# A two-layer block on one core: the recurrent stage fed with x as it stands, its products scaled afterwards

## The reference, cut to what matters

```python
def rg_lru(x, w_r, b_r, w_i, b_i, lam):
    r = sigmoid(block_diag_linear(x, w_r, b_r))
    i = sigmoid(block_diag_linear(x, w_i, b_i))
    log_a = -8.0 * r * softplus(-lam)
    a = exp(log_a)
    u = sqrt(-expm1(2.0 * log_a)) * (i * x)
    # h_t = a_t * h_(t-1) + u_t over the tokens
def hybrid_layer(x, ...):
    h = rmsnorm(x, g_mix)                  # x * rsqrt(mean(x*x) + eps) * g
    z = h @ w_in
    rnn_x, rnn_y, conv_b, conv_c, conv_x, gate_rnn, gate_conv = split(z)
    rnn_x = causal_depthwise_conv(rnn_x, conv4_w) + conv4_b
    y_rnn = gelu(rnn_y) * rg_lru(rnn_x, ...)
    y_conv = conv_b * causal_depthwise_conv(conv_c * conv_x, conv3_w)
    merged = sigmoid(gate_rnn) * y_rnn + sigmoid(gate_conv) * y_conv
    x = x + merged @ w_out
    ...                                    # a gated feed-forward, then an embedding gate
```

## Time and profile before

| what | value |
|---|---|
| median of 3 runs | 976.36 us (975.74 to 976.37) |
| the profiled execution's own time | 975.19 us |
| its span, first to last instruction | 973.4 us |
| PE busy in the span | 942.3 us |
| DVE busy | 741.0 us |
| ACT busy | 622.4 us |
| mean granted TensorE clock | 0.989 of full |
| bytes read from HBM | 213.03 MB |

### The profile page before, as it was taken

The page is one execution under the profiler, slowest core; times in us unless marked ns, Lnnn a source line. Parts: engine busy times, 40 slices in busy tenths (PEclk is TensorE's granted clock), DMA queues, the critical chain, the costliest instruction groups (busy, mean ns, idle before and its releaser), DMA issues.

```text
span 973.4 us, 13805 instructions
## 1 busy us (share of the span) xinstructions
PE 942.3 (97%) x5019; PEld 813.1 (84%) x5019; DVE 741.0 (76%) x1085; ACT 622.4 (64%) x949; POOL 20.5 (2%) x40
## 2 busy tenths in 40 slices
PE   7999999989899999999999799999999999999996
PEld 6888888878788888888888799999997888888875
DVE  5557686368799999999998778889797554555575
ACT  6685684566488877878777856756565643444455
POOL 2400000000000000000000000000000000000000
PEclk9999999999899999999999999999999999999999
DMA  9655325236199999999998264747466555555521
GB/s 339 200 187 199 130 92 212 87 99 223 70 360 368 359 369 370 350 365 371 335 371 305 82 206 148 228 128 237 151 215 203 200 180 183 187 190 174 202 99 43
DMA packets 102651, 214.64 MB, mean 221 GB/s; under 512 B 5629, under 2 KB 60177, under 8 KB 96977
## 3 DMA queue, kind: packets, MB, share of 16 engines
q1 hardware_dynamic: 101056, 211.83, 62.4%
q0 software_dynamic: 1392, 2.20, 0.8%
q10 hardware_dynamic: 160, 0.07, 0.0%
HBM read 213.03 MB, written 1.05 MB: 220 GB/s over the span
## 4 chain that ended last, share of the span: by engine, by line
PE 89%; DVE 5%; ACT 3%; issue 1%; DMA 1%; SPq 0%; DVEq 0%; ACTq 0%
PE bank L2113 21%; PE bank L2115 21%; PE bank L2114 21%; PE bank L2656 6%; PE bank L2657 6%; PE bank L2658 6%; PE bank L2118 4%; DVE w_lo L436 1%; DVE w_lo L438 1%; DMA xs<-in_mem_dram 1%; DVE xT_lo L1456 1%; PE bank L2443 1%; PE bank L2444 0%; ACT arena L924 0%; PE bank L2669 0%
## 5 line engine op out<-in xcount | busy, mean ns | idle before, releaser
L2113 PE MATMUL bank<-w_hi,xT_hi 128*128 128x512 f32 (+1 forms) x704 | 280.5, 398 | 1.6 <-DVE xT_lo L1456 1.0
L2115 PE MATMUL bank<-w_hi,xT_lo 128*128 128x512 f32 (+1 forms) x704 | 274.9, 390 | 0.0
L2114 PE MATMUL bank<-w_lo,xT_hi 128*128 128x512 f32 (+1 forms) x704 | 274.5, 390 | 0.0
L2113 PEld LDWEIGHTS bank<-w_hi,xT_hi 128*128 128x128 f32 x704 | 133.1, 189 | 29.0 <-issue 2.1
L2115 PEld LDWEIGHTS bank<-w_hi,xT_lo 128*128 128x128 f32 x704 | 132.4, 188 | 27.8
L2114 PEld LDWEIGHTS bank<-w_lo,xT_hi 128*128 128x128 f32 x704 | 132.8, 189 | 25.3
L436 DVE TENSOR_TENSOR w_lo<-stage,w_hi 128x1024 fp32r<-128x1024 f32 (+3 forms) x101 | 115.7, 1146 | 36.9 <-ACT w_hi L422 36.0
L2656 PE MATMUL bank<-xT_hi,w_hi 128*128 128x256 f32 x448 | 127.0, 284 | 0.0
L2657 PE MATMUL bank<-xT_lo,w_hi 128*128 128x256 f32 x448 | 126.8, 283 | 0.0
L2658 PE MATMUL bank<-xT_hi,w_lo 128*128 128x256 f32 x448 | 126.8, 283 | 0.0
L422 ACT ACTIVATE w_hi<-stage 128x1024 fp32r<-128x1024 f32 (+3 forms) x102 | 101.8, 998 | 37.3 <-PE bank L2658 18.8
(11 more groups left out here) (405 smaller groups left out, 1358.1 us busy)
## 6 DMA issues: line engine op xcount, KB each, us to landing
stage<-in_w_in_dram SPq DMA_DIRECT2D x36, 1024.0 KB, 5.1
stage<-in_w_gate_up_dram SPq DMA_DIRECT2D x44, 512.0 KB, 4.4
more<-in_expert_w_down_dram SPq DMA_DIRECT2D x17, 1024.0 KB, 6.6
stage<-in_expert_w_gate_dram SPq DMA_DIRECT2D x33, 512.0 KB, 5.1
stage<-in_expert_w_up_dram SPq DMA_DIRECT2D x33, 512.0 KB, 6.1
more<-in_expert_w_gate_dram SPq DMA_DIRECT2D x31, 512.0 KB, 5.0
more<-in_expert_w_up_dram SPq DMA_DIRECT2D x31, 512.0 KB, 5.9
stage<-in_expert_w_down_dram SPq DMA_DIRECT2D x15, 1024.0 KB, 6.7
```

Of the source, the lines that this page charges most:

```text
L2113: mm(o, k_hi, v_hi, start=start, stop=False)
L2114: mm(o, k_hi, v_lo, start=False, stop=False)
L2115: return mm(o, k_lo, v_hi, start=False, stop=stop)
```

## The change

- PE transposes `x` itself, two banks after two of the four additions and two after four. The squares, the mean and `rstd` are taken beside that and behind it. `rstd` is spread to a row of tokens (`row_wide`), transposed by PE inside the first GELU unit into a bank `scales`, and kept as `scale_row` (and its square `scale_row2`) in `xs`.
- In the heads, each product is multiplied by `scale_row` (a tensor_tensor over 512 columns whose second operand is read twice): RX into `xpad` by DVE in place of ACT's copy; GELU into `y_in` by DVE in place of ACT's copy; C times X in `cpad`, by the square, added; B's part in `conv3`, added; the gates G_R and G_C by DVE into `gr_tanh` and `gc_tanh`, which ACT then turns into tanh in place.
- The decay is ACT's Exp of `r_tanh` with scale and bias `decay_rate`, two instructions. On DVE the two reciprocals, the addition before them and the affine step behind them go, and one affine step (`q_inv`) comes. The polynomial of gelu has one tensor_scalar less. The split of G_C stands ahead of the decay's step.
- At the end of the experts, both chunks of the last down weights are split on ACT before the last tanh, and U_HEADS and U_HEADS + 1 (the first RX and GELU) before and behind `aT_hi`; DVE splits U_HEADS whole ahead of `sums`, and U_HEADS + 1 behind the `xT_lo` parts. In `down_by_chunks` and `bring_back` the matmuls that need only high parts come first.
- PE's first head is written out ahead of the loop, which then has three passes. POOL's load of `p_in` waits for the first `rx_hi`.

```diff
@@ ACT, end of the experts
+                if last_down_unit is not None:
+                    for c in range(2):
+                        chunk_hi(act, last_down_unit, c, st)
                 act.wait_ge(st.unit_done, g * PER_TURN + (up_unit(base, j) + 1))
...
-                if last_down_unit is not None:
-                    for c in range(2):
-                        chunk_hi(act, last_down_unit, c, st)
+                if last_down_unit is not None and splits[0]:
+                    splits[0]()
                 act.wait_ge(sem(name + "_turned"), eighths(g, j + 1))
                 nc.scalar.activation(flat3(aT_hi[:])[:, 0:FF], bank[7][:, 0:FF], ACT.Copy).then_inc(sem(name + "_aT_hi"), 1)
+                if last_down_unit is not None and splits[1]:
+                    splits[1]()
@@ ACT, the turn
         warm_up(ACT.Sqrt)
-        for c in range(2):
-            for t in range(T):
...
+        mix_squares(0, 0)
+        high_parts("mix", MIX_G)
+        mix_squares(0, 1)
+        mix_squares(1, 0)
+        mix_squares(1, 1).then_inc(sem("norm_sums"), 1)
         roots("mix")
-        for t in range(T):
-            nc.scalar.activation(xs[:, t, 512:1024], x[:, t, 512:1024], ACT.Copy, scale=rstd[:, t:t + 1]).then_inc(sem("mix_right"), 1)
-        high_parts("mix", MIX_G)
-        split_hi(act, SLOT, U_HEADS + 1)
@@ ACT, the heads
-            done(RX)
-            nc.scalar.activation(xpad[:, :, 3:259], blocks(bank[0]), ACT.Copy).then_inc(sem("rx_copied"), 1)
...
-            nc.scalar.activation(y_sq[:], bank[1][:, :], ACT.Square)
-            nc.scalar.activation(y_in[:], bank[1][:, :], ACT.Copy).then_inc(sem("y_copied"), 1)
+            act.wait_ge(sem("y_scaled"), h + 1)
+            nc.scalar.activation(y_sq[:], y_in[:], ACT.Square, scale=float(np.sqrt(0.044715))).then_inc(sem("y_squared"), 1)
...
+            for f in range(2):
+                rate = decay_rate[:, bass.ds(h * 2 + f, 1)]
+                nc.scalar.activation(decay_a[:, 256 * f:256 * f + 256], r_tanh[:, f], ACT.Exp, scale=rate, bias=rate)
...
-            done(G_R)
-            nc.scalar.activation(gr_tanh[:], bank[5][:, :], ACT.Tanh, scale=0.5).then_inc(sem("gr_tanh"), 1)
+            act.wait_ge(sem("gates_scaled"), h * 2 + 1)
+            nc.scalar.activation(gr_tanh[:], gr_tanh[:], ACT.Tanh, scale=0.5).then_inc(sem("gr_tanh"), 1)
             split_hi(act, SLOT, U_HEADS + 10, UNITS_HEAD, h)
-            done(G_C)
-            nc.scalar.activation(gc_tanh[:], bank[6][:, :], ACT.Tanh, scale=0.5).then_inc(sem("gc_tanh"), 1)
+            act.wait_ge(sem("gates_scaled"), h * 2 + 2)
+            nc.scalar.activation(gc_tanh[:], gc_tanh[:], ACT.Tanh, scale=0.5).then_inc(sem("gc_tanh"), 1)
@@ DVE, the heads
+            def scaled(dst, src, row):
+                return tt(by_feature(dst[:]), by_feature(src[:, :]), over_both(row), ALU.mult)
...
             unit(C_CONV)
+            done(RX)
+            tt(xpad[:, :, 3:259], by_feature(bank[0][:, :]), over_both(scale_row), ALU.mult).then_inc(sem("rx_copied"), 1)
...
-            link(ts(y_sq[:], y_sq[:], 0.044715, 1.0, ALU.mult, ALU.add))
-            tt(y_sq[:], y_sq[:], y_in[:], ALU.mult).then_inc(sem("gelu_inner"), 1)
+            done(GELU)
+            scaled(y_in, bank[1], scale_row).then_inc(sem("y_scaled"), 1)
             unit(RG_R)
+            dve.wait_ge(sem("y_squared"), h + 1)
+            stt(y_sq[:], y_sq[:], 1.0, y_in[:], ALU.add, ALU.mult).then_inc(sem("gelu_inner"), 1)
...
+            link(tt(cpad[:, :, 2:258], cpad[:, :, 2:258], over_both(scale_row2), ALU.mult))
...
+            unit(G_C)
             dve.wait_ge(sem("tau"), h * 2 + 2)
-            tf = tau[:].rearrange("p f t -> p (f t)")
-            link(ts(q_inv[:], tf, 1.0, None, ALU.add))
-            nc.vector.reciprocal(q_inv[:, 0:256], q_inv[:, 0:256])
-            unit(G_C)
-            link(nc.vector.reciprocal(q_inv[:, 256:512], q_inv[:, 256:512]))
-            ts(decay_a[:], q_inv[:], 2.0, -1.0, ALU.mult, ALU.add)
+            ts(q_inv[:], decay_a[:], 0.5, 0.5, ALU.mult, ALU.add)
             split_lo(dve, SLOT, U_HEADS + 9, UNITS_HEAD, h)
+            done(G_R)
+            scaled(gr_tanh, bank[5], scale_row).then_inc(sem("gates_scaled"), 1)
             done(B_CONV)
             y_conv = conv3[:].rearrange("p f t -> p (f t)")
-            tt(y_conv, bank[4][:, :], y_conv, ALU.mult)
+            link(tt(y_conv, bank[4][:, :], y_conv, ALU.mult))
+            tt(conv3[:], conv3[:], over_both(scale_row), ALU.mult)
...
+            done(G_C)
+            scaled(gc_tanh, bank[6], scale_row).then_inc(sem("gates_scaled"), 1)
             split_lo(dve, SLOT, U_HEADS + 10, UNITS_HEAD, h)
@@ PE
-        turn("mix", xs, [("mix_scaled", T)], (0, 1))
-        turn("mix", xs, [("mix_right", T)], (2, 3))
-        pe.wait_ge(sem("x_moe"), 4)
-        with pe.Fori(0, HEADS) as h:
+        turn("mix", x, [("x_moe", 2)], (0, 1))
+        turn("mix", x, [("x_moe", 4)], (2, 3))
...
+        head(0, first=True)
+        with pe.Fori(1, HEADS) as h:
+            head(h)
```

More of the change, by code:

```diff
@@ L1291, in read_flag, with early_head_split @@
             over_flag.append(overflow(act))
-        def early_head_split():
+        def early_head_split(u):
             with act.If(over_flag[0] < 1):
-                split_hi(act, SLOT, U_HEADS)
-        experts("moe", main, U_MOE, GROUPS, 1, read_flag, early_head_split)
+                split_hi(act, SLOT, u)
+        experts("moe", main, U_MOE, GROUPS, 1, read_flag, [lambda u=u: early_head_split(u) for u in (U_HEADS, U_HEADS + 1)])
         with act.If(over_flag[0] > 0):
@@ L1335, in _ @@
             nc.scalar.activation(rx_hi[:], rx[:].rearrange("p f t -> p (f t)"), ACT.Copy).then_inc(sem("rx_hi"), 1)
-            done(GELU)
-            nc.scalar.activation(y_sq[:], bank[1][:, :], ACT.Square)
-            nc.scalar.activation(y_in[:], bank[1][:, :], ACT.Copy).then_inc(sem("y_copied"), 1)
             unit(RG_R)
+            act.wait_ge(sem("y_scaled"), h + 1)
+            nc.scalar.activation(y_sq[:], y_in[:], ACT.Square, scale=float(np.sqrt(0.044715))).then_inc(sem("y_squared"), 1)
+            done(C_CONV)
+            nc.scalar.activation(c_in[:], bank[2][:, :], ACT.Copy).then_inc(sem("c_copied"), 1)
             act.wait_ge(sem("gelu_inner"), h + 1)
             nc.scalar.activation(y_tanh[:], y_sq[:], ACT.Tanh, scale=float(np.sqrt(2 / np.pi))).then_inc(sem("gelu_tanh"), 1)
-            done(C_CONV)
-            nc.scalar.activation(c_in[:], bank[2][:, :], ACT.Copy).then_inc(sem("c_copied"), 1)
             unit(B_CONV)
@@ L1864, in hidden_low @@
                    ALU.subtract).then_inc(sem(name + "_aT_lo"), 1)
-                if last_down_unit is not None:
-                    chunk_lo(dve, last_down_unit, 1, st).then_inc(st.lo_ready, 1)
             def sums(g):
@@ L1952, in _ @@
         dve.wait_ge(sem("padded"), 1)
+        b = product(dve, "scales")
+        then(nc.vector.tensor_copy(scale_row, b[:, 0:256]))
+        ins = tt(scale_row2, scale_row, scale_row, ALU.mult)
+        frees(ins, "scales")
+        been_read(dve, "scales")
         with dve.Fori(0, HEADS) as h:
@@ L2499, in down_by_chunks @@
                 s = u0 % RING
-                pe.wait_ge(sem(name + "_aT_lo"), eighths(g, LAST + 1))
+                hi, lo = (flat3(v[:]) for v in (aT_hi, aT_lo))
                 for c in range(2):
-                    if c:
-                        pe.wait_ge(st.lo_ready, u0 + 1)
+                    o, at = bank[4 + c][:, :], [D * k + 512 * c for k in range(2)]
+                    pe.wait_ge(sem(name + "_aT_hi"), eighths(g, LAST + 1))
                     for k in range(2):
-                        ins = down_block(LAST, s, k, c)
+                        mm(o, hi[:, P * k:P * k + P], w_hi[:, s, at[k]:at[k] + 512], start=False, stop=False)
+                    pe.wait_ge(sem(name + "_aT_lo"), eighths(g, LAST + 1))
+                    pe.wait_ge(st.lo_ready, u0 + 1)
+                    for k in range(2):
+                        mm(o, lo[:, P * k:P * k + P], w_hi[:, s, at[k]:at[k] + 512], start=False, stop=False)
+                        ins = mm(o, hi[:, P * k:P * k + P], w_lo[:, s, at[k]:at[k] + 512], start=False, stop=k == 1)
                     ins.then_inc(st.unit_done if c else sem("last_chunk"), 1)
@@ L2639, in swiglu, with turn_scales, head @@
             down(steps - 1, base + 3 * steps - 1, 0, 0, last_step=True)
-        turn("mix", xs, [("mix_scaled", T)], (0, 1))
-        turn("mix", xs, [("mix_right", T)], (2, 3))
-        pe.wait_ge(sem("x_moe"), 4)
-        with pe.Fori(0, HEADS) as h:
+        turn("mix", x, [("x_moe", 2)], (0, 1))
+        turn("mix", x, [("x_moe", 4)], (2, 3))
+        def turn_scales():
+            pe.wait_ge(sem("row_wide"), 1)
+            b = to_fill(pe, "scales")
+            for t in range(T):
+                ins = transpose(b[:, P * t:P * t + P], row_wide[:, t])
+            fills(ins, "scales")
+        def head(h, first=False):
```

(4 more changed lines are left out.)

78 lines of the change are left out of this document (38 added, 40 removed).

## The result

The changed kernel takes 981.51 us (median of 5 runs, 980.44 to 981.91) against 976.36 before (median of 5, 975.74 to 976.70): a ratio of 1.0052, 95% interval 1.0041 to 1.0064. It is 5.1 us slower, where 975.8 was forecast with a range up to 978.4. The profiled execution has 981.17 us of its own and a span of 979.4, 6.0 above that of before.

What follows compares the result with a forecast made beforehand. PE, busy 97% of the span, was taken to bound the kernel, gaining only where idle or low-clocked. Terms -4.8 + 4.3 = -0.5 against the profiled 975.19; with the median 1.2 above that, 975.8 us, range 971.6 to 978.4.

Steps and rivals of the forecast that it cites:

- Term 1: Turn from experts to heads: xT parts and PE's first unit start earlier; -4.8 us, bounds -4.0 to -5.3.
- step (2): Turn: PE transposes at 541.7 and from 542.95, so the xT_hi parts start at 542.45, 4.8 us earlier.
- Term 2: Heads: PE waits 1.25 us in each of heads 2 to 4, plus 0.3 and 0.24; +4.3 us.
- C: Turn: the norm's chain wasn't what held PE, term 1 given back at the weights' first split; about 980 us, chance 0.02.
- A: Heads: DVE doesn't bind and PE isn't held; 971.8 us, chance 0.19 with what lies between it and the main case.
- D: Heads: the loops bind harder, each missed 0.1 us costing 0.3; 0.8 per head gives 978.2 us, chance 0.10.
- B: Turn: clock falls as PE works in pieces with gaps, costing up to 3.0 us; 978.5 us, chance 0.07.

Runs made afterwards that it cites:

- e11: Kernel before the change with only the split of each next head's third weight unit (C_CONV) moved to the loop's end: 976.62 us.
- e2: Changed kernel with SP's load of the first head's X_CONV weight unit held back until the mixed x is split: 980.53 us.
- e1: Changed kernel with TensorE's branch over the overflow block taken out: 976.29 us.
- e3: Kernel before the change with TensorE's branch over the overflow block taken out: 976.02 us.
- e9: Kernel before the change with the decay part alone: decay by ScalarE's exponential, without the two reciprocals; turn and norm as they were: 975.27 us.
- e13: Changed kernel with the block behind TensorE's branch filled with 240 products in place of the overflow expert's: 981.94 us.
- e4: Changed kernel with TensorE's read of the overflow flag moved ahead of the last expert's steps, the jump left in place: 981.16 us.
- e7: Changed kernel, branch as it is, with the split of each next head's third weight unit (C_CONV) moved to the loop's end: 977.09 us.
- e10: Changed kernel with the two reciprocals put back for the exponential, the norm's factors still applied to the products: 984.84 us.
- e14: Changed kernel with the block behind TensorE's branch filled with 480 products in place of the overflow expert's: 981.83 us.
- e12: Changed kernel with the block behind TensorE's branch filled with 120 products in place of the overflow expert's: 976.92 us.
- e5: Changed kernel with TensorE's branch kept but the block it jumps over cut to its two waits: 976.51 us.
- e6: Changed kernel with TensorE's program behind the branch written twice, so that the no-overflow case falls through and all work is kept: 975.86 us.

## Why the prediction was wrong

**Term 1, the turn (-4.8): failed, at one step.** It was step (2), "PE transposes at 541.7". I took the profile's wait for `xs`, 3.9 us, as all that held PE, and listed what PE needs in data. The instruction ahead of the transposes is a jump over the overflow expert, and neither the chain nor the waits show it as long as a later wait covers it. Its end in the kernel before, about 545.5 by the packet, left 0.6 us to be gained (nothing in e11), and the weight load that the change lets through, worth 0.75 us in e2, takes that back. All else in the step was right: without the jump (e1 against e3) the transposes start 4.45 us earlier (forecast 4.4), the first product 5.00 (forecast 4.8), at a full clock. With the jump, the way from `aT_hi` to the first product is 13.59 us where it was 13.55.

**Term 2, the heads (+4.3): right in mechanism and place, undersized.** From the first product to ACT's first `xT_hi` behind the heads it takes 199.64 us in e1 (from 544.91) and 194.71 in e3 (from 549.91): +4.9.

```profile
744.55 0.85 ACT xT_hi L911 x2
744.62 0.85 ACT xT_hi L901 x2
```

Each loop cost 44.57 - 43.19 = 1.38 in place of 1.25, together 0.4 more. The other 0.2 lies in the first head and at the edges: there PE waits 0.5 us for DVE's splits, where I had 0.3 (and my own two times, 562.4 and 562.2, give only 0.2). The price of 0.12 for the link held: `conv`'s scaling starts 0.72 behind its linked predecessor (634.65, 635.37), where an unlinked one starts 0.60 behind.

**The sum.** -4.8 + 4.3 became 0.0 + 4.85 in the profiles (550.08 to 749.70 against 549.18 to 743.95 for the second). Of the span's 6.0, another 0.86 had come about before the turn: `aT_hi` is written at 535.6 to 536.5 in the four traces with the old turn and at 535.9 to 537.2 in the twelve with the new one, so at least part of this is a difference between executions. What is left, 0.25, lies behind the heads. With the jump out of the way the two terms all but cancel, as forecast: e1 and e3 are 0.3 us apart.

**The rivals.** C, "the norm's chain wasn't what held PE", at about 980, is what happened. I gave it 0.02, since I looked for the other holder among the splits of the weights; its place was wrong there, its size nearly right (term 1 is given back whole, as it has it). A fell (the heads are bound by DVE's chain), D came in small (0.13 per head), and B's low clock did come, but from the idle time and not from gaps in the work: e1 has the gaps and a full clock.

## What to carry to other kernels

A wait in a profile hides whatever ends before it on the same engine's queue, control flow included: before pricing the removal of a wait, list every instruction between the engine's last work and the waiting one, branches too, and ask when each would be through. Let the common case fall through: a jump over a long block that is never executed cost 5 us here once no other wait covered it, over a short one nothing. And before adding steps to an engine with a quarter of its time idle, walk the chain that runs from one iteration to the next, because the free time may stand in waits beside it (VectorE had 3.5 us more to spare in e9 and the loop was no shorter); a step of that chain that can run inside such a wait is the cure.

## What the runs showed of the hardware

- TensorE's jump over 240, 352 or 480 products leaves it idle for 4.6 to 5.1 us with nothing to wait for while a 1 MB load is under way (e13, the changed kernel, e4, e7, e10, e14), and for 3.9 us without the load (e2). Over 120 products or over two waits it is 0.7 and 0.5, the wait for x (e12, e5). A branch that falls through costs nothing that can be seen (e6).
- The clock falls behind such idle time (0.50 from 547 to 550 us), which makes 16 transposes take 3.51 in place of 2.29 us. So a stall of 4.7 us costs more than itself: from `aT_hi` to the first product it is 13.59 us with the jump and 8.65 without (e1), 4.9 more, where PE's idle time ahead of the transposes grows by 4.2.
- One packet of the instruction queue q8 comes 2.6 to 2.8 us ahead of PE's start in every trace in which the long jump holds it, and there is none between 541 and 548 us where PE jumps over nothing or over two waits.
- The jump is 0.75 us shorter when the 1 MB load beside it is held back (e2). That instructions and weights share the DMA engines' time is the likely reason; a run in which only the load's size varies was not made.
- Open: where between 120 and 240 products the step lies, that what is waited for is the code at the target (it fits the step, the packet and e2, but no view names it, and over 120 products the packet comes too, without a stall), and whether the other engines' jumps cost the same; theirs are hidden in all of these kernels.
